# Second attention of a transformer kernel: modulation weights of the next block multiplied four chunks at a time instead of two

## The chip, the cores and the metric

One core of one Trainium2 chip runs the whole program in one launch. The metric is the device time in microseconds (us), lower is better. The program is float32 throughout.

## The reference, cut to what matters

The reference runs two transformer blocks. Of the first one the part that matters is the second attention ("nsa"): 16 heads of 64 over 256 tokens, each with three branches (15 compressed keys, a causal one, a causal windowed one), whose outputs are gated and added. Of the second one it is the modulation vector, which depends on two small vectors alone:

```
# first block, for each head and branch
s = q @ k.T * scale;  p = masked_softmax(s);  o += gate * (p @ v)
# second block
mod   = silu(c)     @ w_ada_2 + b_ada_2     # c: 1 x 1024, w_ada_2: 1024 x 6144
mod_c = silu(c_ctx) @ w_ada_2 + b_ada_2
```

The two products with w_ada_2 need nothing of the attention, and the attention needs nothing of them. They are wanted once the first block is done.

## The kernel before, in words

The program is written out by engine: TensorE (`pe`), ScalarE (`act`), VectorE (`dve`) and the DMA queue of SyncE (`sp`) each have their own list, and semaphores tie them. All weights stream through a ring of six slots of 2 MB in SBUF; `sp` issues the loads in the order of one list and, before each, waits until the slot's former occupant is freed. The list runs ..., `wkv.0` to `wkv.2`, `w1k`, `w1v`, `wq.0` to `wq.2`, `ada2.0` to `ada2.11`, `bout.0`, `bout.1`, then the weights of the first mixture of experts. `ada2.c` is the chunk of 512 columns number c of w_ada_2, 1024 x 512.

The attention runs over 96 units: 16 heads, 2 token tiles of 128 (t), 3 branches (br). A unit has L keys: 15 for br 0, and 128 for t = 0 or 256 for t = 1 in the other two. So L goes 15, 128, 128, 15, 256, 256 and repeats every six units. It is a software pipeline. In turn s:

- TensorE: scores of unit s (L521); what `extra(s)` adds; transposes of the probabilities of unit s-2 (L531), 128 keys at a time; probabilities times values of unit s-3 (L547).
- VectorE: scale and mask (L1495), row maximum (L1496), then for unit s-1 the reciprocal (L1504), the gate (L1506) and the scaling of the probabilities (L1511, or L1509 for br 0).
- ScalarE: exponential of unit s (L1180, with a read of the accumulated sum), copy of the transposed probabilities of unit s-2 to SBUF (L1197), and after every 12 units a copy of the finished head pair (L1201).

Score and transpose results rotate over five PSUM banks (`open_job` waits until the bank's last result is taken). Each float32 matmul shows as two records in the trace.

`extra` is `ada2_step`. It fits the modulation product in between: the two vectors are the stationary operand (2 columns), a chunk's rows stream past, and the result is 2 rows x 512 in PSUM bank 0. Chunks go in pairs p = 0 to 5. In every second turn both chunks of the pair get the product of one k tile (of 8), so a pair takes 16 turns and all six take 96. The rows of the pair's two chunks lie at PSUM partitions 0 and 64, or 32 and 96 for odd pairs (`row_at`), and so on two column tiles of the array. ScalarE then copies the two rows to SBUF (L1188) in turns 0 and 1 of the next pair, TensorE transposes them into columns (L447, four transposes to 2 columns) in turns 2 and 3, and VectorE adds the bias (L1487, `ada2_columns`). The last pair's copies, transposes and bias come after turn 95: the copies of ScalarE in turns 96 and 97, the transposes in turn 98 and in `ada2_step(99)`. A chunk's slot is freed by its last product. After the attention TensorE waits for all heads and multiplies by `bout.0` (L464).

The other attention of the program ("dsa", earlier, 32 units with L 128 and 256 in turn, the same helper and lines) has no `extra`.

Of the kernel before, what the change touches and what calls it, by code (L numbers as in the profile page):

```python
# [16 lines left out]
KT = D // P  # L17
T = 256
NT = T // P
HD = 64  # L20
# [54 lines left out]
def program(nc, A, out):  # L75
    with ExitStack() as ctx:
# [29 lines left out]
        psum = ctx.enter_context(nc.psum_tensor("psum", [P, 8, 512], F32))  # L106
# [146 lines left out]
        place, freed = {}, {}  # L253
# [126 lines left out]

            return (0, P * (t + 1)) if j < MH else (P * t, T)

        def row_at(c):

            return HD * (c % 2) + 32 * (c // 2 % 2)

        def mlstm_units():
            return [(j, t) for j in range(8) for t in range(NT)]

# [21 lines left out]
        def _(pe):  # L411
# [13 lines left out]
            def ada2_step(s):  # L425


                p, k = s // 16, s % 16 // 2
                if p < 6 and s % 2 == 0:
                    if k == 0:  # L430
                        ada2_step.w = [chunk(f"ada2.{c}") for c in (2 * p, 2 * p + 1)]
                        if p >= 2:
                            pe.wait_ge(s_rowc, 2 * p - 2)
                    for i in range(2):
                        r = row_at(2 * p + i)
                        mm = pe.matmul(psum[r:r + 2, 0, :], c2[:, k, :], ada2_step.w[i][:, k, :], start=(k == 0),  # L436
                                       stop=(k == KT - 1), skip_group_check=True)
                        if k == KT - 1:
                            mm.then_inc(s_row, 1)
                            freed[f"ada2.{2 * p + i}"] = (s_row, 2 * p + i + 1)  # L440
                if s >= 18 and (s - 18) % 16 < 2:
                    c = (s - 18) // 16 * 2 + (s - 18) % 16
                    r = row_at(c)
                    b, _ = open_job(pe, "acol", "V")
                    pe.wait_ge(s_rowc, c + 1)
                    for j in range(4):
                        mm = pe.transpose(b[:, 2 * j:2 * j + 2], tmp[r:r + 2, 0, P * j:P * j + P], ident[r:r + 2, r:r + 2])  # L447
                    mm.then_inc(res, 1)
# [63 lines left out]
            def attention(kind, ks, vs, extra=None):  # L512
                units = att_units(kind)
                base = att_base[kind]
                pt = {}
                for s in range(len(units) + 3):
                    if s < len(units):
                        h, t, br, L = units[s]
                        b, _ = open_job(pe, "S", "V")
                        r = (h % 2) * HD  # L520
                        pe.matmul(b[:, 0:L], qT[r:r + HD, h // 2, P * t:P * t + P], ks[br](r, h // 4, L),  # L521
                                  start=True, stop=True).then_inc(res, 1)
                    if extra:
                        extra(s)
                    if 2 <= s < len(units) + 2:
                        h, t, br, L = units[s - 2]
                        b, pt[s - 2] = open_job(pe, "T", "A")
                        pe.wait_ge(s_prob, base + s - 1)
                        for j in range(-(-L // P)):
                            w = min(P, L - P * j)  # L530
                            mm = pe.transpose(b[0:w, P * j:P * j + P], prob[:, (s - 2) % 3, P * j:P * j + w], ident)  # L531
                        mm.then_inc(res, 1)
                    if s >= 3:
                        u = s - 3
                        h, t, br, L = units[u]
                        pair = h // 2
                        first = (h % 2 == 0 and t == 0 and br == 0)
                        if first and pair >= 2:
                            pe.wait_ge(s_otook, base_pair(kind) + pair - 1)
                        pe.wait_ge(*pt.pop(u))  # L540
                        nbr = 1 if kind == "dsa" else 3
                        r = (h % 2) * HD
                        o = psum[r:r + HD, 6 + pair % 2, P * t:P * t + P]
                        nk = -(-L // P)
                        for j in range(nk):
                            w = min(P, L - P * j)
                            mm = pe.matmul(o, vs[br](w, j, h // 4), probT[0:w, u % 2, j, :],  # L547
                                           start=(br == 0 and j == 0), stop=(br == nbr - 1 and j == nk - 1))
                        mm.then_inc(s_pv, 1)
# [350 lines left out]
            for g in range(NKV):  # L900
                for cb in range(2):
# [23 lines left out]
                       lambda r, g, L: kd[r:r + HD, 2, g, 0:L]],  # L925
                      [lambda w, j, g: vc[0:w, g, :], lambda w, j, g: vt[0:w, 0, j, HD * g:HD * g + HD],
                       lambda w, j, g: vt[0:w, 1, j, HD * g:HD * g + HD]], ada2_step)
            ada2_step(99)
            pe.wait_ge(s_otook, 16)
            for n in range(2):  # L930
                w = chunk(f"bout.{n}")
# [137 lines left out]
            units = mlstm_units()  # L1069
# [70 lines left out]
        def _(act):  # L1140
# [32 lines left out]
            def attention(kind):  # L1173
                units, base = att_units(kind), att_base[kind]
                nbr = 1 if kind == "dsa" else 3
                for s in range(len(units) + 3):
                    if s < len(units):
                        h, t, br, L = units[s]
                        act.wait_ge(s_scored, base + s + 1)
                        act.activation(prob[:, s % 3, 0:L], score[:, s % 3, 0:L], ACT.Exp, bias=nmx[:, s % 4:s % 4 + 1],  # L1180
                                       accum_out=rsum[:, s % 4:s % 4 + 1]).then_inc(s_exp, 1)
                    if kind == "nsa" and s >= 16 and s % 16 < 2:
                        c = s // 16 * 2 - 2 + s % 16
                        r = row_at(c)
                        act.wait_ge(s_row, c + 1)
                        if c >= 4:
                            act.wait_ge(*mark["acol"][c - 4])
                        act.activation(tmp[r:r + 2, 0, :], psum[r:r + 2, 0, :], ACT.Copy).then_inc(s_rowc, 1)  # L1188
                    if 2 <= s < len(units) + 2:
                        u = s - 2  # L1190
                        h, t, br, L = units[u]
                        b = next_job(act, "T", "A")
                        if base + u >= 2:
                            act.wait_ge(s_pv, base + u - 1)
                        w = min(P, L)
                        n = -(-L // P)
                        act.activation(probT[0:w, u % 2, 0:n, :], b3(b, 4)[0:w, 0:n, :], ACT.Copy).then_inc(act_took, 1)  # L1197
                    if s >= 3 and (s - 3) % (4 * nbr) == 4 * nbr - 1:
                        pair = (s - 3) // (4 * nbr)
                        act.wait_ge(s_pv, base + s - 2)  # L1200
                        act.activation(oT[:, pair, :], psum[:, 6 + pair % 2, 0:T], ACT.Copy).then_inc(s_otook, 1)  # L1201
# [200 lines left out]
        def _(dve):  # L1402
# [86 lines left out]
            def attention(kind, masks, gate=None):  # L1489
                units, base = att_units(kind), att_base[kind]  # L1490
                for s in range(len(units) + 1):
                    if s < len(units):
                        h, t, br, L = units[s]
                        b = next_job(dve, "S", "V")
                        V(stt(score[:, s % 3, 0:L], b[:, 0:L], SCALE, masks[br][:, t, 0:L], ALU.mult, ALU.add), dve_took)  # L1495
                        V(dve.tensor_reduce(nmx[:, s % 4:s % 4 + 1], score[:, s % 3, 0:L], AX, ALU.max, negate=True), s_scored)  # L1496
                    if kind == "nsa" and s >= 18 and (s - 18) % 16 < 2:
                        ada2_columns((s - 18) // 16 * 2 + (s - 18) % 16)
                    if s >= 1:
                        u = s - 1  # L1500
                        h, t, br, L = units[u]
                        dve.wait_ge(s_exp, base + u + 1)
                        r = rinv[:, u % 4:u % 4 + 1]
                        V(dve.reciprocal(r, rsum[:, u % 4:u % 4 + 1]))  # L1504
                        if gate is not None:
                            V(tt(r, r, gate[:, t, 3 * h + br:3 * h + br + 1], ALU.mult))  # L1506
                        p = prob[:, u % 3, 0:L]
                        if kind == "nsa" and br == 0:
                            V(stt(p, p, r, pk("cmp01", NT)[:, t, :], ALU.mult, ALU.mult), s_prob)  # L1509
                        else:  # L1510
                            V(ts(p, p, r, None, ALU.mult), s_prob)  # L1511
# [294 lines left out]
                V(rope_pair(qT[:, 2 * i:2 * i + 2, :], raw[:, i % 2], mark["raw"][12 + i]), s_rope)  # L1806
            dve.wait_ge(*mark["gates"][0])
            attention("nsa", [pk("cmpneg", NT), causal, causal], gates)
            ada2_columns(10)
            ada2_columns(11)  # L1810
            residual(M(8))
            norm(3, hT, [(uT, G(4))])

# [397 lines left out]
```

## Time and profile before

| | |
|---|---|
| time, median of 3 runs | 2563.54 us (2562.18, 2563.54, 2578.25) |
| profiled execution, time | 2562.28 us |
| profiled execution, span | 2560.5 us |
| TensorE busy | 91% of the span |
| VectorE busy | 29% |
| ScalarE busy | 16% |
| second attention, first score matmul to first matmul by `bout.0` | 693.84 to 862.54 us |
| granted TensorE clock over the span, mean | 0.922 |

The profiled execution's own time is 1.8 us above its span. Busy time of TensorE takes in the modelled end of each record, so a busy TensorE may still be waiting for short times. The granted clock is a share of 2.4 GHz: 1.00 is 2.4 GHz and 0.50 is 1.2 GHz.

### The profile page before, as it was taken

The page shows a single profiled execution, that of the slowest core. Times are in us where ns is not written, and L with a number is a line of the kernel's source. Part 1 is how long each engine was busy: PE and PEld are TensorE (multiplying, and loading weights), DVE is VectorE, ACT ScalarE, POOL GpSimd, SP SyncE. Part 2 cuts the span into 40 slices and gives each one's busy share as a digit, 9 for nine tenths or more (in the row PEclk, how much of TensorE's full clock was granted, in tenths as well). Part 3 has the DMA queues.
Part 4 walks back from the last instruction along what each step waited for, and adds up shares of the span by engine and source line. Part 5 has one row for each costly group of instructions (what it writes and reads, how often), then busy time and mean ns, then how long its engine had stood idle before and what let it go on. Part 6 is the DMA issues. An engine that isn't in the chain of part 4 may idle for free.

```text
span 2560.5 us, 75374 instructions
## 1 busy us (share of the span) xinstructions
PE 2333.3 (91%) x33826; PEld 2005.0 (78%) x33826; DVE 739.4 (29%) x2049; ACT 418.9 (16%) x883; POOL 0.2 (0%) x4
## 2 busy tenths in 40 slices
PE   4979899987999989999999999999979796699996
PEld 3746788876744679999999999999968465577775
DVE  5566644323277320001000000100041244422223
ACT  1022100010144221111011111111121311211111
POOL 0000000000000000000000000000000000000000
PEclk7956999967899989999999999999999978699999
DMA  9330888632334359999999999999951000099994
GB/s 340 129 134 28 315 298 315 248 115 80 132 132 151 146 181 394 352 394 345 394 347 394 345 361 380 345 394 347 394 222 66 1 1 0 7 381 407 407 407 176
DMA packets 253002, 640.76 MB, mean 250 GB/s; under 512 B 15104, under 2 KB 21376, under 8 KB 247680
## 3 DMA queue, kind: packets, MB, share of 16 engines
q1 hardware_dynamic: 252080, 634.93, 66.3%
q10 hardware_dynamic: 848, 4.84, 0.5%
q8 instruction: 46, 0.75, 0.1%
q14 instruction: 28, 0.23, 0.0%
HBM read 638.68 MB, written 1.05 MB: 250 GB/s over the span
## 4 chain that ended last, share of the span: by engine, by line
PE 83%; DVE 7%; DMA 7%; ACT 2%; issue 1%; DVEq 0%; ACTq 0%
PE psum L668 35%; PE psum L464 8%; DMA ring<-in_w_up 6%; PE psum L578 3%; PE psum L565 3%; PE psum L587 3%; PE psum L765 3%; PE psum L521 3%; PE psum L547 3%; PE psum L455 2%; PE psum L436 2%; PE psum L531 2%; PE psum L648 1%; PE psum L421 1%; PE psum L966 1%; PE psum L1116 1%
## 5 line engine op out<-in xcount | busy, mean ns | idle before, releaser
L668 PE MATMUL psum<-uT,ring 128*64 128x96 f32 x14336 | 601.3, 246 | 0.0
L668 PEld LDWEIGHTS psum<-uT,ring 128*64 128x64 f32 x14336 | 594.6, 137 | 0.1
L668 PE MATMUL psum<-arena,ring 128*64 128x96 f32 x7168 | 305.2, 246 | 0.0
L668 PEld LDWEIGHTS psum<-arena,ring 128*64 128x64 f32 x7168 | 299.1, 137 | 0.0
L1574 DVE TENSOR_TENSOR arena<-arena,psum 128x288 f32<-128x288 f32 x56 | 25.5, 455 | 755.8 <-PE psum L668 755.8
L1447 DVE SCALAR_TENSOR_TENSOR arena<-ring,cact,arena 128x512 f32<-128x512 f32 x196 | 147.4, 752 | 7.0
L1242 ACT ACTIVATE arena<-psum 128x384 f32<-128x384 f32 x56 | 27.5, 491 | 738.1 <-PE psum L668 738.1
L464 PE MATMUL psum<-uT,ring 128*128 128x256 f32 (+1 forms) x496 | 112.5, 388 | 6.3 <-ACT uT L1163 6.3
L464 PEld LDWEIGHTS psum<-uT,ring 128*128 128x128 f32 (+1 forms) x496 | 95.6, 193 | 24.5 <-ACT uT L1163 6.7
L464 PE MATMUL psum<-arena,ring 128*128 128x256 f32 x384 | 89.1, 394 | 9.9 <-ACT uT L1163 9.5
L464 PEld LDWEIGHTS psum<-arena,ring 128*128 128x128 f32 x384 | 75.8, 199 | 21.7 <-ACT uT L1163 9.9
L578 PE MATMUL psum<-uT,ring 128*128 128x256 f32 x352 | 80.3, 388 | 6.5 <-ACT uT L1163 6.5
L756 PEld LDWEIGHTS psum<-uT,ring 128*64 128x64 f32 x2432 | 73.7, 138 | 15.0 <-issue 14.2
L521 PE MATMUL psum<-arena 64*128 64x128 f32 (+2 forms) x256 | 81.7, 408 | 2.3 <-DVE arena L1461 2.3
L765 PE MATMUL psum<-uT,ring 128*64 128x64 f32 x2432 | 75.0, 223 | 7.9 <-DMA ring<-in_w_up 7.6
L578 PEld LDWEIGHTS psum<-uT,ring 128*128 128x128 f32 x352 | 68.5, 195 | 16.6 <-issue 6.8
L1144 ACT ACTIVATE arena<-psum 128x512 f32<-128x512 f32 (+2 forms) x63 | 34.9, 554 | 283.2 <-PE psum L464 133.5
L765 PEld LDWEIGHTS psum<-uT,ring 128*64 128x64 f32 x2432 | 72.5, 138 | 9.8 <-DMA ring<-in_w_up 9.7
L531 PEld LDWEIGHTS psum<-pack,prob 128*128 128x128 f32 (+1 forms) x176 | 21.4, 147 | 73.9 <-issue 48.3
L547 PE MATMUL psum<-probT,arena 128*64 128x128 f32 (+1 forms) x352 | 78.1, 334 | 0.2 <-ACT probT L1197 0.2
L587 PE MATMUL psum<-uT,ring 128*128 128x256 f32 x352 | 77.8, 379 | 0.0
L565 PE MATMUL psum<-arena,ring 128*128 128x256 f32 x352 | 77.6, 379 | 0.0
(346 smaller groups left out, 2516.7 us busy)
## 6 DMA issues: line engine op xcount, KB each, us to landing
ring<-in_moe_w_gate SPq DMA_DIRECT2D x224, 512.0 KB, 7.1
ring<-in_moe_w_up SPq DMA_DIRECT2D x224, 512.0 KB, 5.9
ring<-in_moe_w_down SPq DMA_DIRECT2D x224, 512.0 KB, 7.3
ring<-in_w_ada SPq DMA_DIRECT2D x36, 2048.0 KB, 13.7
ring<-in_w_gate SPq DMA_DIRECT2D x19, 2048.0 KB, 10.9
ring<-in_w_up SPq DMA_DIRECT2D x19, 2048.0 KB, 11.4
ring<-in_w_down SPq DMA_DIRECT2D x19, 2048.0 KB, 10.0
ring<-in_ffn_w_gate SPq DMA_DIRECT2D x5, 2048.0 KB, 8.5
```

The source lines that it names most:

```text
L436: mm = pe.matmul(psum[r:r + 2, 0, :], c2[:, k, :], ada2_step.w[i][:, k, :], start=(k == 0), stop=(k == KT - 1), skip_group_check=True)
L464: mm = pe.matmul(b[0:rows, T * j:T * j + T], wt[:, k, c0 + P * j:c0 + P * j + rows], X[:, k, :], start=(k == 0), stop=(k == kt - 1))
L521: pe.matmul(b[:, 0:L], qT[r:r + HD, h // 2, P * t:P * t + P], ks[br](r, h // 4, L), start=True, stop=True).then_inc(res, 1)
L531: mm = pe.transpose(b[0:w, P * j:P * j + P], prob[:, (s - 2) % 3, P * j:P * j + w], ident)
L547: mm = pe.matmul(o, vs[br](w, j, h // 4), probT[0:w, u % 2, j, :], start=(br == 0 and j == 0), stop=(br == nbr - 1 and j == nk - 1))
L565: mm = pe.matmul(psum[:, 4 + j // 2, T * (j % 2):T * (j % 2) + T], down.w[:, 2 * (h % 2) + f, P * j:P * j + P], hid[:, h % 2, f, :], start ...
L578: mm = pe.matmul(psum[:, h % 2, T * f:T * f + T], ffn.g[:, k, 256 * (h % 2) + P * f:256 * (h % 2) + P * f + P], X[:, k, :], start=(k == 0) ...
L587: mm = pe.matmul(psum[:, 2 + h % 2, T * f:T * f + T], ffn.u[:, k, 256 * (h % 2) + P * f:256 * (h % 2) + P * f + P], X[:, k, :], start=(k = ...
L668: mm = pe.matmul(out(HD * hc), w[:, c0 + HD * hc:c0 + HD * hc + HD], x, skip_group_check=True, **kw)
L756: mm = pe.matmul(psum[HD * hc:HD * hc + HD, 0, N * f:N * f + N], w[:, k, o:o + HD], M.xg[:, k, :], start=(k == 0), stop=(k == KT - 1), ski ...
L765: mm = pe.matmul(psum[HD * hc:HD * hc + HD, 1, N * f:N * f + N], w[:, k, o:o + HD], M.xg[:, k, :], start=(k == 0), stop=(k == KT - 1), ski ...
L1447: V(stt(acc, w[:, k, :], cact[:, k:k + 1], acc, ALU.mult, ALU.add), s_acc if k == KT - 1 else None)
```

## The change

The modulation chunks go in groups of four instead of pairs: p = 0, 1, 2, each over 32 turns. In turns 0, 3, 6, ... 21 of a group all four chunks get the product of one k tile, at PSUM partitions 0, 32, 64 and 96, so on four column tiles of 32. Turns 22 to 31 have no product. ScalarE copies the four rows in turns 25 to 28, TensorE transposes them in turns 27 to 30, and VectorE adds the bias in the same turns. So the last group is finished in turn 94, inside the attention, and what followed the last unit is gone. Chunks are now freed four at a time in turn 21 of each group; chunks 4 to 7 are wanted together in turn 32 and 8 to 11 in turn 64.

```diff
-                p, k = s // 16, s % 16 // 2
-                if p < 6 and s % 2 == 0:
+                p, k = s // 32, s % 32 // 3
+                if s % 32 % 3 == 0 and k < KT:
                     if k == 0:
-                        ada2_step.w = [chunk(f"ada2.{c}") for c in (2 * p, 2 * p + 1)]
-                        if p >= 2:
-                            pe.wait_ge(s_rowc, 2 * p - 2)
-                    for i in range(2):
-                        r = row_at(2 * p + i)
-                        mm = pe.matmul(psum[r:r + 2, 0, :], c2[:, k, :], ada2_step.w[i][:, k, :], start=(k == 0),
+                        ada2_step.w = [chunk(f"ada2.{4 * p + i}") for i in range(4)]
+                        if p:
+                            pe.wait_ge(s_rowc, 4 * p)
+                    for i in range(4):
+                        mm = pe.matmul(psum[32 * i:32 * i + 2, 0, :], c2[:, k, :], ada2_step.w[i][:, k, :], start=(k == 0),
                                        stop=(k == KT - 1), skip_group_check=True)
                         if k == KT - 1:
                             mm.then_inc(s_row, 1)
-                            freed[f"ada2.{2 * p + i}"] = (s_row, 2 * p + i + 1)
-                if s >= 18 and (s - 18) % 16 < 2:
-                    c = (s - 18) // 16 * 2 + (s - 18) % 16
-                    r = row_at(c)
+                            freed[f"ada2.{4 * p + i}"] = (s_row, 4 * p + i + 1)
+                if 27 <= s % 32 < 31:
+                    i = s % 32 - 27
+                    r = 32 * i
                     b, _ = open_job(pe, "acol", "V")
-                    pe.wait_ge(s_rowc, c + 1)
+                    pe.wait_ge(s_rowc, 4 * p + i + 1)
...
-            ada2_step(99)
...
-                    if kind == "nsa" and s >= 16 and s % 16 < 2:
-                        c = s // 16 * 2 - 2 + s % 16
-                        r = row_at(c)
+                    if kind == "nsa" and s < len(units) and 25 <= s % 32 < 29:
+                        c = s // 32 * 4 + s % 32 - 25
+                        r = 32 * (c % 4)
                         act.wait_ge(s_row, c + 1)
...
-                    if kind == "nsa" and s >= 18 and (s - 18) % 16 < 2:
-                        ada2_columns((s - 18) // 16 * 2 + (s - 18) % 16)
+                    if kind == "nsa" and s < len(units) and 27 <= s % 32 < 31:
+                        ada2_columns(s // 32 * 4 + s % 32 - 27)
...
-            ada2_columns(10)
-            ada2_columns(11)
```

## Rows read from the trace of the kernel before

**Rows 1.** The page's busy times: share of the span, instructions
```profile
PE 2333.3 (91%) x33826; PEld 2005.0 (78%) x33826; DVE 739.4 (29%) x2049; ACT 418.9 (16%) x883; POOL 0.2 (0%) x4
```

**Rows 2.** The chain that ended last, 690 to 866 us, shares by line
```profile
by line: PE psum L436 25.2%; PE psum L521 24.2%; PE psum L547 23.9%; PE psum L531 15.5%; PE psum L447 2.5%; PE psum L464 2.0%; issue 1.4%; DVE score L1495 0.8%; DVE nmx L1496 0.8%; PE psum L499 0.5%; DVE tmp L1459 0.4%; DVE tmp L1460 0.4%; 
```

**Rows 3.** Groups of instructions by shape, 694 to 860 us: busy, mean, idle before
```profile
L436 PE MATMUL psum<-ring,cact 128*2 128x512 f32 x192 | 50.4, 603 | 0.0
...
L1180 ACT ACTIVATION_READ_ACCUMULATOR prob<-score,nmx 128x1 f32 x96 | 17.9, 186 | 0.0
L1180 ACT ACTIVATE prob<-score,nmx 128x256 f32<-128x256 f32 x32 | 16.3, 508 | 40.3 <-DVE nmx L1496 40.3
...
L1504 DVE RECIPROCAL rinv<-rsum 128x1 f32<-128x1 f32 x96 | 15.7, 164 | 3.4
L1506 DVE TENSOR_TENSOR rinv<-rinv,gates 128x1 f32<-128x1 f32 x96 | 15.3, 160 | 3.3
...
L1495 DVE SCALAR_TENSOR_TENSOR score<-psum,pack 128x256 f32<-128x256 f32 x32 | 13.6, 425 | 12.9 <-PE psum L521 12.5
L1496 DVE TENSOR_REDUCE nmx<-score 128x1 f32<-128x256 f32 x32 | 13.4, 420 | 1.1
...
L1511 DVE TENSOR_SCALAR prob<-prob,rinv 128x256 f32<-128x256 f32 x32 | 11.3, 353 | 1.1
...
L1495 DVE SCALAR_TENSOR_TENSOR score<-psum,pack 128x128 f32<-128x128 f32 x32 | 9.3, 292 | 7.5 <-PE psum L521 5.7
L1511 DVE TENSOR_SCALAR prob<-prob,rinv 128x128 f32<-128x128 f32 x32 | 9.2, 287 | 1.1
L1496 DVE TENSOR_REDUCE nmx<-score 128x1 f32<-128x128 f32 x32 | 9.2, 286 | 1.2
...
L1509 DVE SCALAR_TENSOR_TENSOR prob<-prob,rinv,pack 128x15 f32<-128x15 f32 x32 | 7.5, 234 | 1.1
...
L1495 DVE SCALAR_TENSOR_TENSOR score<-psum,pack 128x15 f32<-128x15 f32 x32 | 5.6, 174 | 11.6 <-PE psum L521 11.0
L1496 DVE TENSOR_REDUCE nmx<-score 128x1 f32<-128x15 f32 x32 | 5.4, 169 | 1.1
```

**Rows 4.** TensorE in order of time: start, length, instructions
```profile
739.45 0.39 PE L521 MATMUL psum<-arena 64*128 64x15 f32 x2
...
741.01 1.03 PE L436 MATMUL psum<-ring,cact 128*2 128x512 f32 x4
741.97 0.33 PE L531 MATMUL psum<-pack,prob 128*128 128x128 f32 x1
...
749.47 0.39 PE L521 MATMUL psum<-arena 64*128 64x15 f32 x2
```

**Rows 5.** Stretches: length, busy of PE, PEld, DVE, ACT, POOL, granted clock, DMA
```profile
163.00:225.00 62.00, 62.00 (x177) 33.34 (x177) 32.99 (x111) 23.00 (x88) 0.00 (x0) 0.50 0.00 1
...
694.00:698.00 4.00, 4.00 (x14) 1.25 (x14) 1.85 (x9) 0.89 (x4) 0.00 (x0) 0.60 1.04 388
698.00:855.00 157.00, 155.86 (x775) 71.64 (x773) 112.67 (x472) 73.59 (x294) 0.00 (x0) 1.00 0.38 137
```

**Rows 6.** Score line of the other attention, 163 to 225 us
```profile
L521 PE MATMUL psum<-arena x55: 417/627/792, 163.3 to 224.9; 64*128 64x256 f32 x28, 64*128 64x128 f32 x27
```

**Rows 7.** Issue of ada2.8 and ada2.9, and landing times of those two loads
```profile
745.16 1.00 SPq L2023 DMA_DIRECT2D ring<-in_w_ada  x2
...
DMA to landing us min/median/max: 9.3/11.7/14.2
```

**Rows 8.** ScalarE and TensorE in order of time after the last unit's scores
```profile
857.91 0.59 ACT L1188 ACTIVATE tmp<-psum 2x512 f32<-2x512 f32 x1
...
860.44 0.58 PE L447 MATMUL psum<-pack,tmp 2*128 2x2 f32 x4
...
862.54 3.63 PE L464 MATMUL psum<-arena,ring 128*128 128x256 f32 x9
```

More of the change, by code:

```diff
@@ L381, in srange @@
             return (0, P * (t + 1)) if j < MH else (P * t, T)
-        def row_at(c):
-            return HD * (c % 2) + 32 * (c // 2 % 2)
         def mlstm_units():
@@ L522, in attention @@
                                   start=True, stop=True).then_inc(res, 1)
-                    if extra:
+                    if extra and s < len(units):
                         extra(s)
```

## The prediction, made before the changed kernel ran

> **What bounds the kernel now.** I read the page's busy times first: TensorE is busy for 91% of the span [rows 1], so time is won where TensorE gets less to do and nothing else takes its place. The chain of the stretch around the change says the same: the modulation products hold 25.2% of it, the scores 24.2%, the values 23.9%, the transposes 15.5%, and VectorE's two score lines 0.8% each [rows 2]. To be seen there: in this attention the four TensorE lines follow each other, and the modulation products lie in the open, not in gaps.
>
> The groups of instructions give the count: 192 records of the products, 50.4 us busy, no idle time before them [rows 3]. That is 48 steps of four records (two chunks, two records each). Read in order of time, a step begins at 741.01 and the transpose behind it at 741.97: 0.96 us a step [rows 4]. A record takes 603 ns in the mean [rows 3], so the four in a row would need about twice the 0.96 us; the two column tiles already run side by side. The change therefore does not bring in this overlap, it widens it from two to four.
>
> The same view gives the period. Six units (L = 15, 128, 128, 15, 256, 256) go by between the scores at 739.45 and those at 749.47: 10.02 us [rows 4], 1.67 us a unit. Three steps lie in it, 2.88 us, so TensorE needs 7.14 us for six units by itself, 1.19 a unit.
>
> Now VectorE, the next engine in the loop, for six units, from the means by shape [rows 3]: L1495 2 x (174 + 292 + 425) = 1782 ns; L1496 2 x (169 + 286 + 420) = 1750; L1504 6 x 164 = 984; L1506 6 x 160 = 960; the scaling 2 x (234 + 287 + 353) = 1748. Sum 7.22 us. The idle time before each instruction that waits for nothing is some 34 ns (1.1 us before 32) [rows 3]; thirty of them make 1.02, so 8.25 us. VectorE also waits for the exponential of a 256-key unit (508 ns and part of the 186 of the read) when the unit behind it has 15 keys (174 + 169 ns and gaps): about 0.25 us, and less behind a 128-key unit. I take 8.6 us for six units, 1.44 a unit; between 8.25 and 8.9. So without steps this loop does not run at TensorE's 1.19 but at VectorE's 1.44.
>
> **The change part by part.** The sum is made against the profiled execution, 2562.28 us, which is 1.3 us below the median of 2563.54.
>
> *Steps, 48 of two chunks to 24 of four.* If four tiles run side by side, a step stays at 0.96 us. It can't be less, since each record still streams 512 columns. If the tiles go two by two, it is 1.92. The nearest row is the pair's own, where the second tile costs nothing, so I take 0.96. Small extra weight loads are hidden or worth some 0.02 each.
>
> *Turns 0 to 23 of each group, 72 units with a step every third.* TensorE needs 1.19 + 0.96 / 3 = 1.51 a unit, above VectorE's 1.44: 72 x 1.51 = 108.7 us. *The other 24 units have no step*: VectorE sets 1.44: 34.5 us (33.0 to 35.6). Together 143.2 against 96 x 1.67 = 160.3: 17.1 us less. Of the 23 us of TensorE work removed, 6 go to VectorE as a new wait.
>
> *Row copies, transposes, bias.* They move, their number stays 12. ScalarE's copy is 0.59 us [rows 8]. It stands between the exponential of s and the copy for s-2, now in four turns in a row. ScalarE then holds about 0.51 + 0.19 + 0.36 + 0.59 us, near 1.65, above VectorE's 1.44. TensorE's four transposes hold it up 0.51 at the half clock [rows 8], about 0.3 at the full one; VectorE gets one short addition more. Each is as dear as before, where it sat on TensorE's path, or hidden up to 0.3: between 0 and 3 us less. I take 1, for the copies make new waits of about the same size.
>
> *The tail.* Before, two row copies (2 x 0.59) and two sets of transposes (2 x 0.51) lay among the last transposes and values, and `bout.0` began at 862.54 [rows 8]. Half of that was on the path: 1.1 of 2.2 us; between 0.5 and 2.2.
>
> *Chunks.* Chunks 6 and 7 go into slots that now come free in turn 21, and turn 32 wants them. Behind a free pair the first load lands after 9.3 us and the second after 14.2, issued within 1 us [rows 7], so the pair is there 15 us later. From the end of step 21 to step 32 TensorE passes 11 units, 11 x 1.44 = 15.8, and four row turns with 0.2 or more each: 16.6. Cover 1.6 us, so nothing; were the units as short as TensorE allows (1.19), the wait would be about 1 us, twice. Chunks 8 and 9 are queued behind and wanted 30 units later. Chunks 2 and 3 are wanted 16 turns earlier than before, but their slots were freed by `w1v` and `wq.0`, and both land ahead of the attention; chunks 4 and 5 were issued before it too. `bout` and the experts' weights are freed earlier than before, never later.
>
> *The start.* The clock is low for most of the first 4 us (0.60 in the mean [rows 5]) and two steps lay there, now one or little more: 0.5 less.
>
> Sum with nothing else: 17.1 + 1 + 1.1 + 0.5 = 19.7 less, 2542.6, or 2543.9 beside the median.
>
> **The clock.** This is where I choose. The windows show two attentions through the same helper. In the one with a step every second unit the granted clock is 1.00 (2.4 GHz) for 157 us on end, while in the one without steps it is 0.50 (1.2 GHz) for all of 62 us, though TensorE counts as busy throughout [rows 5]. What TensorE did in the latter was short records and waits. Turns 22 to 31 of each group will look like that for some 16 us: short matmuls and VectorE's and ScalarE's waits between them. So I expect the clock to fall there, and to come back after the long products resume, as it did between 694 and 698, where the mean was 0.60 with two steps and then 1.00 [rows 5].
>
> What it costs: the attention at half clock passes 55 records, 27.5 units, in 62 us [rows 5, 6], 2.25 a unit with 1.5 blocks of 128 keys; ours has 8 blocks in six units, so 2.25 x 1.33 / 1.5 = 2.0. A group of three units with its step is then 3 x 2.0 + 1.9 = 7.9 against 4.5: 3.4 us each. A fall costs the last three or four quiet units 0.4 more each, 1.4, and one to two such groups, 3.4 to 6.8; I take 1 + 4 = 5. Two falls lie inside the attention; the third meets the tail, where the clock fell before as well. Two times 5 is 10: 19.7 becomes 9.7, and the time 2552.6, with the median's 1.3 about 2554.
>
> The Trainium skill ("TensorE: Matmul & The Clock Gate", section "Why this matters for your kernels") gives three column tiles side by side 2.38 times the speed of one, not 3 times, which is 0.79 of the ideal. As an estimate by that page, the same shortfall on our step makes 0.96 / 0.79 = 1.21 us, 24 x 0.25 = 6 us more, and 2560 in place of 2554. The pair's row shows no such loss for the second tile, and no row here has three or four.
>
> **The rivals.**
> - *Nothing falls.* Occasional waits of VectorE are short and the clock holds at 1.00: 2544. For it: at the full clock the other units keep TensorE near its path. Against it: the quiet turns, where four ScalarE copies in a row stretch the units.
> - *The tiles go two by two* (so the change does not do what it says). A group of three with a step takes 3 x 1.19 + 1.92 = 5.49; 24 of them 131.8, and 34.5 quiet: 166.3, 6.0 more than before; less 1.1 and 0.5 and 1: 2566, with the median's offset 2567, and up to 2578 with falls of the clock. Against it: pairs overlap fully now.
> - *The clock falls and stays down: slower.* A step every third unit is less than one every second, and from the first quiet stretch on TensorE would stay at 1.2 GHz. 16 groups of three x 3.4 = 54, and 24 quiet units x 0.4 = 10, against 19.7 won: 44 us more, 2607. It decides where the steps, now a third of the turns, no longer bring the clock back. For it: the 62 us at 0.50 without a rise [rows 5]. Against it: one step is 1.9 us of unbroken streaming at that clock.
>
> **How the numbers follow.** A change below 1% is about what a measurement of this kernel can't tell from none; here that is 26 us. Even with no wait at all the removed steps and the tail give only about 25. Chances: falls of the clock with recovery 0.45 (2548 to 2562), nothing falls 0.27 (2540 to 2547), two by two 0.14 (2563 to 2578), stays down 0.09 (2590 and more), something better than I see, as other stages gaining by earlier loads, 0.05. The likeliest gives 2554. The range 2541 to 2575 leaves out the slow rival and the edges. Faster by over 1% (below 2538) 0.05, slower by over 1% (above 2589) 0.09, within 0.86.
>
> **What would show it.** In the changed profile: 192 records of the products as before, eight in about 1 us (right) or 1.9 (two by two). Units of 1.5 us in turns 0 to 23 and 1.4 to 1.7 in turns 24 to 31, where VectorE's and ScalarE's lines should enter the chain. The granted clock of three stretches near turns 26 to 36. Landing of chunk 7 ahead of turn 32, else a wait for DMA on the products' line. No transposes to two columns behind the last unit. I'd be wrong above all if the clock behaves otherwise than in the two attentions shown, or if VectorE's loop is shorter than its sum of means.

## The result and the profile after

The changed kernel takes 2631.53 us (median of 4 runs, 2601.79 to 2632.78) against 2562.86 (4 runs, 2561.37 to 2578.25). The ratio of the means is 1.0226, 95% interval [1.0144, 1.0308], so the changed kernel is 1.4 to 3.1% slower; the medians alone give 1.027. The forecast was 2554, so the sign was wrong too.

| | before | after |
|---|---|---|
| profiled execution, time | 2562.28 us | 2632.18 us |
| span | 2560.5 us | 2630.4 us |
| second attention, first scores to `bout.0` | 693.84 to 862.54, 168.7 us | 695.9 to 931.17, 235.3 us |
| granted TensorE clock, mean of the span | 0.922 | 0.883 |

66.6 of the 69.9 us lie in the changed attention. The page of the changed kernel (span, busy times, the clock in 40 slices):

```profile
span 2630.4 us, 75374 instructions
...
PE 2398.3 (91%) x33826; PEld 2039.9 (78%) x33826; DVE 738.8 (28%) x2049; ACT 421.6 (16%) x883; POOL 0.2 (0%) x4
...
PEclk7956999976756579999999999999998968699999
```

The instruction counts are those of [rows 1], and VectorE and ScalarE are busy as long as before within 3 us; TensorE is busy 65 us longer, with the same instructions. The four slices from 658 to 921 us read 7, 5, 6, 5 in the clock. The stretches say it in numbers (columns as in [rows 5]):

```profile
698.00:814.00 116.00, 114.46 (x385) 53.28 (x387) 55.85 (x235) 36.91 (x144) 0.00 (x0) 0.50 0.23 83
...
698.00:925.00 227.00, 220.67 (x790) 105.29 (x788) 114.80 (x482) 78.37 (x300) 0.00 (x0) 0.55 0.31 112
```

Where before had 1.00 for 157 us, the clock is now 0.50 for 116 us on end, and 0.55 in the mean of the attention. The first 4 us of the attention, counted from its first scores, are the place to look. Before and after:

```profile
693.84:697.84 4.00, 4.00 (x14) 1.41 (x14) 1.72 (x8) 0.89 (x4) 0.00 (x0) 0.62 1.05 388
...
695.88:699.88 4.00, 2.89 (x15) 1.43 (x15) 1.71 (x8) 0.90 (x4) 0.00 (x0) 0.62 1.04 386
```

Both kernels come to their first scores at 1.00, behind a wait of TensorE of 2.29 us, and in both the clock falls about 1 us later, at 694.8 and 696.9. Before, TensorE was then busy without a break, with two steps, and the clock was back at 698.2, 3.4 us after its fall. Now TensorE is busy for 2.89 of the 4 us, with one step, and the clock stays at 0.50 until 816.3, the end of turn 47.

TensorE in order of time, inside the stretch at 0.50:

```profile
731.47 0.61 PE L516 MATMUL psum<-arena 64*128 64x15 f32 x2
732.01 1.89 PE L431 MATMUL psum<-ring,cact 128*2 128x512 f32 x8
733.83 0.48 PE L526 MATMUL psum<-pack,prob 128*128 128x128 f32 x1
...
734.85 1.22 PE L516 MATMUL psum<-arena 64*128 64x256 f32 x2
...
737.02 1.22 PE L516 MATMUL psum<-arena 64*128 64x256 f32 x2
...
739.11 0.61 PE L516 MATMUL psum<-arena 64*128 64x15 f32 x2
```

Three units take 7.64 us (731.47 to 739.11), and the next three 8.07 (to 747.18). The step of eight records lasts 1.82 us, to 733.83; that alone would look like tiles going two by two, but it is the half clock. At the full clock of the first experiment eight records take 0.97 us:

```profile
708.62 1.04 PE L436 MATMUL psum<-ring,cact 128*2 128x512 f32 x8
709.59 0.33 PE L533 MATMUL psum<-pack,prob 128*128 128x128 f32 x1
```

That is the 0.96 us of four records before [rows 4]. The four column tiles run fully side by side.

### The profile page after: what moved, and what is told of

The parts are those of the page before. It is cut to its first block, busy times and chain, and to the rows that moved or that the text cites. A ratio compares the mean times of both kernels' runs of the same rounds, so it can differ in the third digit from the quotient of the medians.

```text
span 2630.4 us, 75374 instructions
## 1 busy us (share of the span) xinstructions
PE 2398.3 (91%) x33826; PEld 2039.9 (78%) x33826; DVE 738.8 (28%) x2049; ACT 421.6 (16%) x883; POOL 0.2 (0%) x4
## 4 chain that ended last, share of the span: by engine, by line
PE 83%; DVE 7%; DMA 6%; ACT 2%; issue 1%; DVEq 0%; ACTq 0%
PE psum L663 34%; PE psum L459 8%; DMA ring<-in_w_up 6%; PE psum L516 4%; PE psum L542 3%; PE psum L573 3%; PE psum L582 3%; PE psum L560 3%; PE psum L760 3%; PE psum L526 2%; PE psum L450 2%; PE psum L431 2%; PE psum L643 1%; PE psum L417 1%; PE psum L960 1%; PE psum L1110 1%
## 5 line engine op out<-in xcount | busy, mean ns | idle before, releaser
L663 PEld LDWEIGHTS psum<-uT,ring 128*64 128x64 f32 x14336 | 594.5, 137 | 0.1
L516 PE MATMUL psum<-arena 64*128 64x128 f32 (+2 forms) x256 | 108.3, 521 | 2.3 <-DVE arena L1455 2.3
L542 PE MATMUL psum<-probT,arena 128*64 128x128 f32 (+1 forms) x352 | 103.1, 423 | 0.0
L459 PE MATMUL psum<-arena,ring 128*128 128x256 f32 x384 | 88.8, 394 | 10.4 <-ACT uT L1157 9.5
L516 PEld LDWEIGHTS psum<-arena 64*128 64x128 f32 x256 | 60.0, 291 | 41.9 <-issue 30.0
L573 PE MATMUL psum<-uT,ring 128*128 128x256 f32 x352 | 80.4, 388 | 6.5 <-ACT uT L1157 6.5
L751 PEld LDWEIGHTS psum<-uT,ring 128*64 128x64 f32 x2432 | 74.0, 138 | 13.5 <-issue 12.4
L526 PE MATMUL psum<-pack,prob 128*128 128x128 f32 (+1 forms) x176 | 65.2, 426 | 19.9 <-DVE prob L1505 18.5
L1174 ACT ACTIVATE prob<-score,nmx 128x128 f32<-128x128 f32 (+1 forms) x128 | 53.7, 419 | 179.6 <-DVE nmx L1490 179.5
```

Source lines behind the costliest of these rows:

```text
L459: mm = pe.matmul(b[0:rows, T * j:T * j + T], wt[:, k, c0 + P * j:c0 + P * j + rows], X[:, k, :], start=(k == 0), stop=(k == kt - 1))
L573: mm = pe.matmul(psum[:, h % 2, T * f:T * f + T], ffn.g[:, k, 256 * (h % 2) + P * f:256 * (h % 2) + P * f + P], X[:, k, :], start=(k == 0) ...
L663: mm = pe.matmul(out(HD * hc), w[:, c0 + HD * hc:c0 + HD * hc + HD], x, skip_group_check=True, **kw)
L751: mm = pe.matmul(psum[HD * hc:HD * hc + HD, 0, N * f:N * f + N], w[:, k, o:o + HD], M.xg[:, k, :], start=(k == 0), stop=(k == KT - 1), ski ...
```

## The experiments

Three theories were on trial. A: the loss is the granted clock. B: every third turn is too sparse to hold it at all. C: the loss is waits in the VectorE and ScalarE loop, at whatever clock. "Zero products" are matmuls by a matrix of zeros, either written where nothing reads or adding zero, so they cost TensorE time and change no output. Turns are numbered from 0, as in the code, by the start of their scores; "kernel 1" is the kernel of experiment 1. The ratios are against the kernel before as run beside each of them (median 2563.65 us for 1 to 4, 2564.44 for 5 to 8, 2564.49 for 9 to 11).

**1. Zero products at the start** (`e1_warm`)

```diff
                         extra(s)
+                        if s in (1, 2):
+                            filler(2)
...
             rope_unit("pair", 15)
+            filler(5)
```

`filler(n)` issues n zero products of 256 columns; the five lie in the 2.3 us wait before the first scores.

> The changed kernel with products by a zero matrix where TensorE waits before the first score matmul (five of 256 columns, 2.1 us) and in turns 1 and 2 of the attention (two each); they are written where nothing reads. Theory A (the loss is the granted clock, and it was lost at the start of the attention): the clock holds at 1.00 through the first 20 turns or more, which saves 24 units x (2.65 - 1.5) = 27 us; it falls in turns 22 to 31: 2590 to 2610 us. Theory B (a step every third turn is too little to hold the clock at all): it falls within a few turns in any case, 2625 to 2640. Theory C (the loss is waits on VectorE and ScalarE, not the clock): no change, 2630.

Measured: 2607.21 us, ratio 1.0173 [1.0154, 1.0192]. The stretches:

```profile
694.00:722.00 28.00, 26.46 (x149) 12.07 (x147) 19.39 (x82) 11.51 (x48) 0.00 (x0) 1.00 0.20 74
723.00:760.00 37.00, 36.56 (x130) 18.84 (x129) 19.33 (x83) 14.29 (x52) 0.00 (x0) 0.50 0.63 227
786.00:804.00 18.00, 16.89 (x96) 8.52 (x96) 14.13 (x60) 9.14 (x38) 0.00 (x0) 1.00 0.31 106
```

The time is in A's range, about 24 us back for nine small matmuls. But the clock did not wait for the quiet turns: it fell at 722.6, in turn 17, where steps still came every third turn. So B has a part: steps every third turn hold the clock for a while, not safely. The stretch at 1.00 also gives what the changed attention does at the full clock. Scores of the two turns that start a period of six units (turns 3 and 9), of this kernel, and the stretch between them:

```profile
698.53 0.39 PE L521 MATMUL psum<-arena 64*128 64x15 f32 x2
...
708.30 0.39 PE L521 MATMUL psum<-arena 64*128 64x15 f32 x2
...
698.53:708.30 9.77, 9.06 (x53) 4.42 (x52) 7.08 (x30) 4.24 (x19) 0.00 (x0) 1.00 0.08 30
```

9.77 us for six units, against 10.02 before [rows 4] and 9.06 (6 x 1.51) in the prediction. The same six units took 15.70 us in the changed kernel at 0.50 (700.06 to 715.76): this is the price of the clock with the order of work unchanged. TensorE is busy for just the 9.06 us of the prediction; the other 0.71 are waits for VectorE. So in this group, even with the clock, the change gains 0.25 us per six units, not 0.96. VectorE shows why, one period later, and TensorE two turns after that step:

```profile
711.01 0.42 DVE L1497 SCALAR_TENSOR_TENSOR score<-psum,pack 128x256 f32<-128x256 f32 x1 [1.10 <-PE psum L521]
711.47 0.42 DVE L1498 TENSOR_REDUCE nmx<-score 128x1 f32<-128x256 f32 x1
711.92 0.16 DVE L1506 RECIPROCAL rinv<-rsum 128x1 f32<-128x1 f32 x1
712.12 0.16 DVE L1508 TENSOR_TENSOR rinv<-rinv,gates 128x1 f32<-128x1 f32 x1
712.32 0.23 DVE L1511 SCALAR_TENSOR_TENSOR prob<-prob,rinv,pack 128x15 f32<-128x15 f32 x1
712.59 0.42 DVE L1497 SCALAR_TENSOR_TENSOR score<-psum,pack 128x256 f32<-128x256 f32 x1
...
712.70 0.27 PE L533 MATMUL psum<-pack,prob 128*15 128x128 f32 x1 [0.54 <-DVE prob L1511]
```

VectorE waits 1.10 us for scores queued behind a step, then works with gaps of 0.04 us only, and TensorE waits 0.54 us for it two turns on.

Steps do not meet the same units in each group. In turns 0 to 21 they fall on units of 15 keys; in turns 32 to 53 they fall on units of 128 and 256 keys. Kernel 1 was at 1.00 there for a while, and its turns 47 and 53 begin at:

```profile
786.28 0.70 PE L521 MATMUL psum<-arena 64*128 64x256 f32 x2
...
795.70 0.70 PE L521 MATMUL psum<-arena 64*128 64x256 f32 x2
```

That is 9.42 us for six units, so in the second group 0.60 us of the 0.96 arrive.

**2. Also in the quiet turns** (`e2_warm_fill`)

```diff
                         b, pt[s - 2] = open_job(pe, "T", "A")
+                        if kind == "nsa" and s % 32 >= 22 and s < len(units):
+                            for _ in range(1):
+                                pe.matmul(b[0:2, 256:512], zeros[:, 0:2], pk("causal")[:, 0:256], ...)
```

This is one zero product of 256 columns a turn, written into the bank of the transposes that follow.

> As the one before, and in turns 22 to 31 of each group one zero product of 256 columns ahead of the transposes, where TensorE waits for VectorE. Theory A: the clock stays at 1.00 from the first unit to the last and the time is what the prediction had without a fall, 2543 to 2552 us, faster than the kernel before. Theory B: 2610 to 2640. Theory C: some 4 us slower than the changed kernel, 2635.

Measured: 2610.09 us, ratio 1.0202 [1.0164, 1.024]. Both A's number and its premise failed, and the time is at the edge of B's range: the clock fell in turn 17 again, before the first added product, and then these products ran at 1.2 GHz and cost time (turns 22 to 31 took 19.8 us, against 14.1 in kernel 1, both at 0.50). Later in the kernel, where the clock was up at the start of the quiet turns, it held through them at 1.00 (798 to 834 us):

```profile
723.00:797.00 74.00, 73.80 (x257) 32.35 (x258) 33.96 (x143) 24.04 (x90) 0.00 (x0) 0.55 0.32 114
798.00:834.00 36.00, 35.17 (x193) 17.04 (x192) 25.74 (x108) 17.63 (x67) 0.00 (x0) 1.00 0.63 227
```

**3. The kernel before with most products left out** (`e3_before_last_k`)

```diff
-                if p < 6 and s % 2 == 0:
-                    if k == 0:
+                if p < 6 and s % 16 == 14:
+                    if k == KT - 1:
...
-                        mm = pe.matmul(..., start=(k == 0), ...)
+                        mm = pe.matmul(..., start=True, ...)
```

> The kernel before without 7 of 8 modulation products of each pair (only the last k tile's is left, so the modulation of the second block is incomplete); rows, transposes and bias stay. 42 steps x 0.96 us of TensorE work are gone. Theory A: the clock is 0.50 nearly all through the attention, 2.0 us a unit, so 2585 to 2600 us, slower though work was taken out. Theory C (VectorE's loop sets the pace without steps, clock or not): 1.44 a unit, 2540 to 2546.

Measured: 2589.92 us, ratio 1.01 [1.0082, 1.0118], as A said, outside C's 2540 to 2546. Its attention:

```profile
695.13:907.81 212.68, 203.78 (x649) 110.21 (x649) 117.30 (x491) 79.16 (x308) 0.00 (x0) 0.53 0.34 123
```

This is the plainest run: 40 us of TensorE work less, nothing added and nothing moved, and 26 us slower at a clock of 0.53. The whole time even hides part of it. The attention itself takes 212.7 us instead of 168.7, 44 us more; but the modulation of the second block is incomplete here, so its tokens go to other experts, and the rest of the program is 16.5 us shorter (1681.4 us behind the attention, against 1697.9; 352 TensorE records less besides the 168 of the steps).

**4. Each step doubled** (`e4_double`)

```diff
+                    for i in range(4):
+                        pe.matmul(psum[32 * i:32 * i + 2, 0, :], zeros[:, 0:2], ada2_step.w[i][:, k, :], start=(k == 0), ...)
                     for i in range(4):
-                        mm = pe.matmul(..., start=(k == 0), ...)
+                        mm = pe.matmul(..., start=False, ...)
```

> The changed kernel with each step doubled by a zero product of the same four tiles (0.86 us more of TensorE work per step at the full clock, 20.6 us in all). Theory A: a step is now as long as two of before, the clock rises after the start as it did before, may fall in the quiet turns and rises again: 2565 to 2585 us, so 50 us faster with more work. Theory C: 2630 + 20 = 2650 or more.

Measured: 2610.22 us, ratio 1.0191 [1.015, 1.0232]. 21 us faster than the changed kernel with 20 us more work, so C is out; the time is 25 us above the upper end of A's range.

```profile
694.00:902.00 208.00, 195.29 (x980) 90.83 (x973) 114.85 (x482) 77.91 (x300) 0.00 (x0) 0.78 0.33 122
```

The clock fell at the start as in the changed kernel, came up in the step of turn 3 (at 700.9), fell for short times among the steps (turn 18 the first) and for 20 us and more in the quiet turns; 0.78 in the mean.

**5. Steps every second turn** (`e5_dense`)

```diff
-                p, k = s // 32, s % 32 // 3
-                if s % 32 % 3 == 0 and k < KT:
+                p, k = s // 32, s % 32 // 2
+                if s % 2 == 0 and k < KT:
```

> The changed kernel with the same 24 steps of four chunks in every second turn: turns 0, 2, ... 14 of each group of 32, and no step in turns 16 to 31. Theory A' (the clock follows how closely the long products stand; every second turn brings it up and holds it, every third does neither for long, none loses it): 1.00 in turns 0 to 15 of each group but for a few microseconds, 0.50 in most of the quiet turns: 48 x 1.67 + 48 x 1.9 = 171 us of attention, 2575 to 2590 us. Rival (the number of steps alone counts): as the changed kernel, 2600 to 2632.

Measured: 2592.54 us, ratio 1.0109 [1.009, 1.0128], 39 us below the changed kernel with the same matmuls, none added; 2.5 us above the range of A' and clear of the rival's. The clock follows the steps:

```profile
700.00:723.00 23.00, 22.64 (x133) 10.54 (x132) 16.64 (x70) 9.86 (x44) 0.00 (x0) 1.00 0.11 33
724.00:757.00 33.00, 32.40 (x111) 18.86 (x114) 18.80 (x80) 13.64 (x50) 0.00 (x0) 0.50 0.61 223
758.00:785.00 27.00, 25.87 (x157) 11.96 (x153) 18.73 (x78) 11.22 (x48) 0.00 (x0) 1.00 0.09 26
786.00:832.00 46.00, 45.56 (x158) 24.03 (x157) 24.15 (x102) 17.09 (x64) 0.00 (x0) 0.50 0.43 160
```

It fell in turns 17 and 48, three and two turns after the last steps of the first two groups, and was back in turns 32 and 68. At the very start, with steps in turns 0 and 2 as in the kernel before, it fell at 696.3 and was back at 699.7, 3.4 us later, as it was there. So how closely the steps stand matters, and not only their number: these steps are those of the changed kernel, only closer. Once down, it took from one step to three.

**6. Steps every second turn, with small zero products in the quiet turns** (`e6_dense_fill`: the start of 1, but in turn 1 only, and one product of 128 columns in turns 16 to 31)

> As e5, with zero products before the first unit (2.1 us, in a wait) and in turn 1, and one zero product of 128 columns ahead of the transposes in each of the quiet turns 16 to 31. Theory A': the clock stays at 1.00, 48 x 1.67 + 48 x 1.5 = 152 us of attention, 2552 to 2560 us. If 128 columns are too few, it falls in the quiet turns and the time is that of e5.

Measured: 2586.26 us, ratio 1.0081 [1.0058, 1.0105], between the two outcomes expected. In the first group the clock held through turn 27 and fell in turn 28, among the row copies and transposes of turns 25 to 30; in the second it fell in turn 49, at once; in the third it held until turn 94, the last with transposes:

```profile
837.00:877.90 40.90, 40.10 (x234) 20.49 (x232) 30.32 (x128) 20.58 (x81) 0.00 (x0) 1.00 0.49 181
```

128 columns a turn hold it in one group and not in another.

**7. Control: the start's zero products in the kernel before** (`e7_before_warm`: as 6, without the quiet turns)

> The kernel before with the same zero products before the first unit and in turn 1. Theory A': only the 3.4 us at the half clock at the start go, 1 to 3 us less: 2560 to 2563. A control: zero products by themselves do neither harm nor more good.

Measured: 2562.67 against 2564.44 us, ratio 0.9989 [0.9979, 0.9999]. As expected: the 3.4 us at half clock are gone and nothing else changes. It is the fastest version here, by 0.1%, too little to matter.

**8. Every third turn, more zero products** (`e8_warm_fill_more`: the start of 1, one of 256 columns in the turn ahead of each step, one of 128 in turns 22 to 31)

> The changed kernel (steps every third turn) with the zero products at the start, one of 256 columns in the turn ahead of each step and one of 128 columns in turns 22 to 31. Theory A': the clock stays at 1.00 throughout; units take 1.63 (measured in the first 16 turns of e1) to 1.7 and 1.6 in the quiet turns: 158 us, 2556 to 2562 us. That is 70 us faster than the changed kernel with 34 zero products more, but no gain on the kernel before: the steps saved are not won, since VectorE sets the pace between them. Rival (no VectorE limit): 2545.

Measured: 2575.13 us, ratio 1.007 [1.0038, 1.0102], 13 us above A' (which counted 34 added products; there are 60). The clock held through all steps of the first group and fell in turns 29, 61 and 93, the third of the four turns with transposes each time:

```profile
694.00:741.00 47.00, 46.67 (x266) 21.88 (x259) 33.22 (x139) 21.67 (x87) 0.00 (x0) 1.00 0.33 120
742.00:752.00 10.00, 10.00 (x42) 4.61 (x41) 5.20 (x22) 3.36 (x13) 0.00 (x0) 0.50 1.05 387
```

**9. And twice as many in the last eight turns of each group** (`e9_fill_double`: in turns 22 and 23 one, in 24 to 31 two, of 256 columns)

> The changed kernel with zero products at the start, one of 256 columns in the turn ahead of each step and in turns 22 and 23, and two of 256 columns in turns 24 to 31, where in e6 and e8 the clock fell when row copies and transposes came. Theory A': now the clock holds at 1.00 from the first unit to the last. 72 units x 1.67 (turns 3 to 20 of e8) and 24 x 2.1: 171 us of attention, 2568 to 2575 us: all of the loss but for the added products is back. If it falls in spite of them, 2580 or more.

Measured: 2576.2 us, ratio 1.0038 [1.0023, 1.0053], 55 us below the changed kernel and 1.2 us above the range. One row for the whole attention:

```profile
693.00:869.00 176.00, 174.21 (x952) 80.42 (x951) 115.10 (x485) 77.69 (x302) 0.00 (x0) 1.00 0.41 147
```

1.00 throughout. The attention takes 181.4 us, against 235.3 in the changed kernel and 168.7 before. The order of steps, copies, transposes and chunk loads is the changed kernel's; with 84 zero products more, the clock is back.

**10 and 11. Without VectorE's gate multiplication**, in kernel 1 and in the kernel before

```diff
-                        if gate is not None:
+                        if False:
                             V(tt(r, r, gate[:, t, 3 * h + br:3 * h + br + 1], ALU.mult))
```

> e1 without VectorE's gate multiplication (0.16 us and a gap per unit; the branches are added ungated). To be read in turns 3 to 15, where e1 had the clock at 1.00 and 9.78 us per six units. Theory V (VectorE's loop sets the pace of the turns without a step, TensorE that of the turns with one, and neither makes up for the other): the turns with a step stay at 2.1, the four others lose 0.19 each: 9.0 us per six units. If TensorE or a fixed delay set the pace, 9.7 or more.

> The kernel before without the same multiplication. Theory V: TensorE sets the pace there, six units stay at 10.0 us and the time within 3 us of before (2560 to 2565). If VectorE sets it there too, 6 x 0.19 less per six units, 18 us in all.

The branches added ungated send other tokens to other experts (36958 TensorE records in 11 against 33826), so the whole times (2734.90 and 2698.74 us, one run each) say nothing here, and my expectation of 2560 to 2565 for 11 overlooked that. To be read is the attention. Kernel 10, scores six units apart at the full clock:

```profile
697.26 0.39 PE L521 MATMUL psum<-arena 64*128 64x15 f32 x2
...
706.71 0.39 PE L521 MATMUL psum<-arena 64*128 64x15 f32 x2
```

9.45 us against 9.77: one multiplication each came off the two turns ahead of a step (1.62 to 1.46 and 1.35 to 1.19, from the second score record of one turn to that of the next), and the other four turns stayed. So VectorE sets two turns of six, not four as I expected, and TensorE the rest. In kernel 11 the clock is 1.00, and six units take 9.88 us (739.64 to 749.52) against 10.02: TensorE sets the pace there, but for 0.14 us.

## Why the prediction was wrong, point by point

**The clock: the step that failed.** The prediction named the mechanism, that units without steps would look to the clock like the attention that runs at 0.50, and it had "the clock falls and stays down" as its slow rival (0.09, 2607). It took as likeliest that the clock falls only in the quiet turns and is back after one to two groups of three. Three parts of that were wrong. First, the start: "one or little more" of a step in the first 4 us was booked as a gain of 0.5 us, but without the second step the clock, once fallen, did not come back. With steps in turns 0 and 2 it was back after 3.4 us, before the change and in kernel 5; with steps in turns 0 and 3, and TensorE busy 2.89 of the first 4 us, it was not until 816.3. Zero products in the wait and in turns 1 and 2 kept it from falling and gave 24 us (1). Second, recovery, the term of "one to two such groups" after a fall: the row used for it had steps every second turn. With every third the kernel stayed at 0.50 for over 116 us; with every second it came back in all three groups (5). Third, holding: even from the full clock it was lost in turn 17 (1, 2), and in turn 11 in kernel 10, before any quiet turn. So the term "two times 5 is 10" measured at least 55. With the clock at 1.00 throughout, all else as changed, 55 us of 69 were back, and the remaining 12 stand against the 75 zero products among the units, which lengthen a turn where the wait is shorter than they are (one in kernel 8 from 1.35 to 1.65 us) (9). That the clock is the cause is shown by 3 and 9 from both sides, and by the same six units at 15.70 and 9.77 us.

The slow rival had the right size for a group of three with a step at half clock: it put it at 7.9 us, and the trace has 7.64 and 8.07 in turn. Its 2607 was low mainly because it let the clock fall in the first quiet turns and not at the start; the eight groups before them, 8 x 3.4 = 27 us by its own price, would have made it 2634. That this meets the measured 2632 is partly luck, for two more of its terms were off, in opposite ways: a quiet unit was to cost 0.4 us more at half clock (and even its own 2.0 against 1.44 makes 0.56), while turns 22 to 31 took 2.30 us each (750.55 to 773.57); and the clock was back at 1.00 for some short stretches behind 816 us.

**Turns 0 to 23.** The sum took the larger of two averages, TensorE 1.51 and VectorE 1.44, thus 1.51 a unit. TensorE's part was right (9.06 us busy in six units), but the units took 1.63 us in the first group and 1.57 in the second at the full clock (1). Turns are not averages: with a step TensorE sets the turn, at 2.1 us, and VectorE idles 1.10; ahead of the next step, in the first group, VectorE sets it, at 1.35 and 1.62, and that idle time can't be used. Of 0.96 us saved in six units 0.25 arrive in the first group and 0.60 in the second. The best this change could have brought at the full clock is, as an estimate from kernel 1, 24 x 0.04 for the first group and 24 x 0.10 for the second, something between for the third, which no run shows at the full clock without added products, and 24 x (1.67 - 1.42) for the quiet turns (turns 54 to 57 took 1.42 on average): 4 to 6, and 6, and the tail's 1, so 11 to 13 us, not 19.7.

**The steps.** Right: 0.97 us for eight records, four tiles side by side. The rival "two by two" is out, and so is the 1.21 us estimated from the Trainium skill ("TensorE: Matmul & The Clock Gate", section "Why this matters for your kernels").

**The tail.** From the last unit's scores to `bout.0`: 7.13 us before (855.41 to 862.54), 7.40 after (923.77 to 931.17), but now at the half clock throughout. In kernel 9, at the full clock, the same stretch takes 5.39 us (869.11 to 874.50), two zero products in it. That is 1.7 less than before, where the clock fell to 0.50 at 858.6; so a saving is seen, but how much of the 1.7 is the clock was not tried apart, and the expected 1.1 us is neither shown nor refuted.

**Chunks.** Of no account here, where the slow turns left more time for the loads: step 32 followed its scores as the others did, and no row of waits has the products wait for a DMA. In kernel 9, at the full clock, turn 32 took 2.18 us and turn 35 2.17, so no wait there either; its turns are longer than those the prediction counted with.

**The range.** Its two ends came from a clock that holds and from clocks that recover. The base of the slow rival was one row of an attention at 0.50 for 62 us, and that was the row nearest to the case.

## What to carry to other kernels

Before TensorE work is taken out of a stretch, look at what the granted clock is there and in the nearest stretch without that work; if the two differ, price the stretch at both, beginning with its first microseconds, and let recovery count only where a row shows it at the same density of work. When a step is made rarer rather than shorter, add up turn by turn which engine ends each one, since a larger average of two engines holds only if the pipeline can store work from one turn to the next. A version with the same products closer together, or a few products by zeros in a wait, shows in one run whether the clock is at stake. Where a kernel leaves out or alters values that steer later work, read the changed stretch and not the whole time (3, 10 and 11).

## What was not expected of the hardware

- Taking 40 us of matmuls out of an unchanged order made the kernel 26 us slower and its attention 44 (3), and adding zero products made the changed one 55 us faster (9).
- The clock's course is not the same in each execution: the four runs of the changed kernel have mean clocks of 0.883, 0.895, 0.884 and 0.888 and times of 2632.18, 2601.79, 2630.89 and 2632.78 us. The fastest is the one with the highest clock. Kernel 8 spreads from 2570.85 to 2594.58; kernel 9, at 1.00 throughout in its trace, from 2573.92 to 2580.53.
- Four column tiles of 32 with four different moving operands of 128 x 512 take 0.97 us for eight records at the full clock, no more than two tiles for four, and 1.82 at the half.
- The clock fell with no long wait before it: in kernel 1, where it fell at 722.6, TensorE had waited at most 0.55 us at a time since its first scores, while it was busy for 26.46 of the 28 us from 694 to 722.
- What exactly makes the clock fall or rise is left open: no run here isolates it. That it fell in the turns with transposes to two columns in every group of kernel 8 and in two of three in kernel 6 is seen; whether these or ScalarE's copies stretch the turns was not tried apart.
